# Hybrid decoder step on one core: dense split in place, merged gathers, earlier pick matrix, reordered end

## The reference

```python
# layer 0: RG-LRU mixer, memory attention, dense SwiGLU; layer 1: gated DeltaNet, memory attention, experts
for i in range(DEPTH):
    mix = rglru(x) if i % 2 == 0 else gated_delta(x)
    x = layer_norm(ALPHA * x + mix)
    x = layer_norm(ALPHA * x + mem_attention(x))
    ff = swiglu(x) if i % 2 == 0 else moe_ffn(x)
    x = layer_norm(ALPHA * x + ff)

def moe_ffn(x):                      # top 2 of 8 experts, softmax over the two logits
    gate = sum(one_hot(top_i) * softmax(top_v))
    return sum(gate[:, e] * swiglu_e(x) for e in range(8))
```

## Time and profile before

| | us |
|---|---|
| timed runs, median of 3 (lowest to highest) | 2506.08 (2505.19 to 2506.25) |
| the profiled execution | 2509.16 |
| its span, first to last instruction | 2507.3 |

### The profile page before, as it was taken

How to read it: one execution, slowest core, us unless ns; L and a number is a source line. 1 busy time by engine, 2 the same in 40 slices (tenths; PEclk the granted TensorE clock), 3 DMA queues, 4 the chain that set the end, 5 groups by cost and what they waited for, 6 DMA issues and landing times.

```text
span 2507.3 us, 43919 instructions
## 1 busy us (share of the span) xinstructions
PE 2291.6 (91%) x17238; PEld 2165.0 (86%) x17238; DVE 1134.6 (45%) x1739; ACT 720.5 (29%) x1218; POOL 1063.6 (42%) x1483
## 2 busy tenths in 40 slices
PE   8998889899999998999999778888799999999993
PEld 8988867899999996888888667867699999999993
DVE  3684412411011147777777644412557777410004
ACT  2352321311001114333333311321355666411103
POOL 4657434588888875433333105534221232100001
PEclk9999899899999998999999988999699999999996
DMA  7214442222222222211121102541176777778884
GB/s 296 100 60 162 154 165 85 93 84 84 89 88 84 89 90 69 69 55 62 62 63 63 45 27 88 194 165 68 52 256 208 260 249 264 238 247 280 285 285 161
DMA packets 98515, 347.22 MB, mean 138 GB/s; under 512 B 13488, under 2 KB 18864, under 8 KB 93472
## 3 DMA queue, kind: packets, MB, share of 16 engines
q1 hardware_dynamic: 73136, 279.08, 31.9%
q10 hardware_dynamic: 19472, 45.28, 5.2%
q0 software_dynamic: 5728, 20.38, 2.2%
HBM read 318.25 MB, written 26.47 MB: 137 GB/s over the span
## 4 chain that ended last, share of the span: by engine, by line
PE 64%; issue 15%; DVE 9%; POOL 6%; ACT 3%; DMA 3%; ACTq 0%; DVEq 0%; POOLq 0%; SPq 0%
PE ps L625 26%; PE ps L1262 8%; PE ps L1235 6%; PE ps L865 4%; PE ps L1264 4%; POOL wl L531 3%; PE ps L1252 3%; POOL wh L527 2%; DMA raw<-weights 2%; PE ps L726 1%; DVE x L1953 1%; PE ps L1076 1%; PE ps L1072 1%; PE ps L1055 1%; PE ps L730 1%
## 5 line engine op out<-in xcount | busy, mean ns | idle before, releaser
L527 POOL TENSOR_TENSOR wh<-raw,tab 128x256 fp32r<-128x256 f32 x672 | 438.8, 684 | 807.4 <-PE ps L625 543.5
L531 POOL TENSOR_TENSOR wl<-raw,wh 128x256 fp32r<-128x256 f32 x672 | 522.1, 808 | 0.0
L625 PE MATMUL ps<-xh,wh 128*128 128x272 f32 x2048 | 306.5, 300 | 47.1 <-POOL wl L531 15.5
L625 PEld LDWEIGHTS ps<-xh,wh 128*128 128x128 f32 x2048 | 276.8, 195 | 61.9 <-issue 24.5
L625 PE MATMUL ps<-xh,wl 128*128 128x272 f32 x2048 | 298.7, 296 | 0.0
L625 PE MATMUL ps<-xl,wh 128*128 128x272 f32 x2048 | 281.0, 289 | 0.0
L625 PEld LDWEIGHTS ps<-xh,wl 128*128 128x128 f32 x2048 | 277.1, 195 | 1.8 <-issue 0.5
L625 PEld LDWEIGHTS ps<-xl,wh 128*128 128x128 f32 x2048 | 266.2, 189 | 0.0
L1262 PE MATMUL ps<-moe_x,moe_wh 128*128 128x416 f32 (+3 forms) x768 | 214.5, 356 | 4.8 <-DVE moe_wl L2458 3.5
L2458 DVE TENSOR_TENSOR moe_wl<-raw,moe_wh 128x1024 fp32r<-128x1024 f32 x144 | 178.1, 1237 | 52.1 <-ACT moe_wh L1832 49.1
L1264 PE MATMUL ps<-moe_x,moe_wl 128*128 128x208 f32 (+3 forms) x768 | 188.9, 246 | 0.0
(11 more groups left out here) (407 smaller groups left out, 3901.4 us busy)
## 6 DMA issues: line engine op xcount, KB each, us to landing
raw<-weights SPq DMA_DIRECT2D x488, 512.0 KB, 4.2
moe_h<-cache SPq DMA_DIRECT2D x6, 2048.0 KB, 8.6
moe_h<-cache ACTq DMA_DIRECT2D x4, 2048.0 KB, 14.9
work<-cache SPq DMA_DIRECT2D x4, 2048.0 KB, 8.0
moe_h<-rows_x POOLq DMA_DIRECT2D x12, 512.0 KB, 8.1
rows_x<-lnsq ACTq DMA_DIRECT2D x9, 512.0 KB, 11.1
work<-scratch ACTq DMA_DIRECT2D x16, 272.0 KB, 4.2
work<-cache ACTq DMA_DIRECT2D x2, 2048.0 KB, 10.4
```

The lines of the kernel that those rows point to most:

```text
L527: nc.gpsimd.tensor_tensor(flat(h1[:, k0:k1]), flat(r1[:, k0:k1]), one_col, MUL).then_inc(pool_hi, 1)
L531: low = nc.gpsimd.tensor_tensor(flat(l1[:, k0:k1]), flat(r1[:, k0:k1]), flat(h1[:, k0:k1]).bitcast(F), SUB)
L625: last = mm(ps[:, 2 * i + h, 0:HT], w[:, par_, k, :], a[:, k, h * HT:(h + 1) * HT], start=(n == 0 and k == 0), stop=(n == 2 and k == KT - 1))
```

## The change

The change has four parts.

Split in place: `wl` now lies on `raw`, so the low part overwrites the tile that it was made from, and `wh` has four tiles. Every load waits for `w_used` of four tiles back. In the query, output, feed-forward and delta-net-output groups (`ahead=True`) `split` waits for the load alone; elsewhere it stays two tiles behind PE. The down loop of the feed-forward is written out twice, since its slot index now depends on the turn.

```diff
-RAW, SPLIT, PIECES = 4, 2, 4
+RAW, PIECES, PACE = 4, 4, 2
...
-        wh = sb("wh", [P, SPLIT, KT, P], R)
-        wl = sb("wl", [P, SPLIT, KT, P], R)
+        wl = nc.alloc_sbuf_tensor_at("wl", [P, RAW, KT, P], R, offset=nc.sbuf_base - 4 * RAW * KT * P)
+        wh = sb("wh", [P, RAW, KT, P], R)
...
-                    if offset is None:
-                        ge(sp, w_used, t * RAW + (j + 1 - RAW))
-                    else:
-                        ge(sp, w_split, t * RAW + (j + 1 - RAW - offset))
+                    ge(sp, w_used, t * RAW + (j + 1 - RAW))
...
                     pool.wait_ge(w_in[j], t * 16 + 16)
-
-                    ge(pool, w_used, t * RAW + (j + 1 - SPLIT - (first if j < SPLIT else 0)))
-                    h1, l1, r1 = wh[:, j % SPLIT], wl[:, j % SPLIT], raw[:, j]
+                    if not ahead:
+                        ge(pool, w_used, t * RAW + (j + 1 - PACE - (direct if j < PACE else 0)))
+                    h1, l1, r1 = wh[:, j], wl[:, j], raw[:, j]
...
-            turns(S_Q[0], 16, 4, 20)
-            turns(S_FFN, HALVES * 36, 4, 24)
-            turns(S_GDN, 4 * GH + 8, 4, 28)
-            turns(S_Q[1], S_MOE - S_Q[1], 4, 32)
+            turns(S_Q[0], 16, 4, 20, ahead=True)
+            turns(S_FFN, HALVES * 36, 4, 24, ahead=True)
+            turns(S_GDN, 4 * GH, 4, 28)
+            turns(S_GDN + 4 * GH, 8, 0, 28, ahead=True)
+            turns(S_Q[1], S_MOE - S_Q[1], 4, 32, ahead=True)
```

```diff
+                    if r == NE - 1:
+                        continue
                     pool.wait_ge(m_ye, KT * (r + 1))
                     pool.dma_start(rows_y[b:b + P, :], M_y[:, 0, :]).then_inc(m_out, 16)
...
-                pool.wait_ge(m_out, OUT_BY[NE - 1])
+                pool.wait_ge(m_x, NE - 1)
+                pool.wait_ge(m_out, OUT_BY[NE - 2])
...
-                            out=Y_in[tt][m][0:n, :], out_offset=None, in_=rows_y,
-                            in_offset=bass.IndirectOffsetOnAxis(ap=R_slot[0:n, m, tt:tt + 1], axis=0)).then_inc(c_in_y[tt], 16)
+                            out=Y_in[tt][m][0:n, :], out_offset=None, in_=rows_y[0:BASE[NE - 1], :],
+                            in_offset=bass.IndirectOffsetOnAxis(ap=Z_slot[0:n, m, tt:tt + 1], axis=0)).then_inc(c_in_y[tt], 16)
...
+            def last_products(tt):
+
+                n = P if tt < NC else NS
+                for hf in range(2):
+                    if tt >= 2:
+                        pe.wait_ge(c_stat, tt - 1)
+                    last = mm(ps[0:n, 4 + 2 * (tt % 2) + hf, :], Z_turned[:, tt * P:tt * P + n], M_y[:, 0, 512 * hf:512 * hf + 512],
+                              start=True, stop=True)
+                last.then_inc(r_pe, 1)
...
+                    if r == NE - 1 and f == 4:
+                        dve.wait_ge(r_pe, SHARED_T + 1)
+                        s(V.tensor_copy(Z_turned[:, 0:TP], ps[:, 6, :]))
+                        s(V.tensor_copy(Z_turned[:, TP:T], ps[:, 7, 0:NS]), r_dve, SHARED + 2)
+                    if r == NE - 1 and f >= FT - NT:
+                        combine(f - (FT - NT))
```

```diff
-                    if tt:
-                        columns(tt - 1)
+                    if tt >= 2:
+                        columns(tt - 2)
+                columns(NT - 2)
                 columns(NT - 1)
...
-                    for m in range(2):
-                        s(V.scalar_tensor_tensor(z, Y_in[tt][m][0:n, :], R_w[0:n, tt, 1 - m:2 - m], z, MUL, ADD))
+                    dve.wait_ge(r_pe, SHARED_T + tt + 2)
+                    z = T_x[0:n, tt, :].rearrange("p (a b) -> p a b", b=512)
+                    s(V.tensor_tensor(z, z, ps[0:n, 4 + 2 * (tt % 2):6 + 2 * (tt % 2), :], ADD))
```

More of the change, by code:

```diff
@@ L42 @@
 ZEROS = -(-ROWS // P)
+SHARED, SHARED_T = 11, 6
 PICKED, GATHERED = 6, 2
@@ L869, in one @@
                     pe.sem_inc(passed, 1)
[L870 to L875 removed]
+                    down(0)
+                    down(1)
                 repeat(pe, n, one)
@@ L1869, in columns @@
                 n = P if tt < NC else NS
-                for hf in range(2):
+                for hf in range(2 if tt < 2 else 1):
                     act.wait_ge(c_tr, 2 * tt + hf + 1)
```

152 lines of the change are left out of this document (100 added, 52 removed).

## The result

The changed kernel takes 2488.5 us in the median (2487.3 to 2493.4) beside 2505.6 us for the kernel before (2504.3 to 2506.3). The ratio is 0.9936 with a 95% interval of 0.9919 to 0.9953: 16 us are won, between 12 and 20. Forecast were 36 us and 2470.2, with a range of 2456 to 2485; the time lies above the range. The sign is right, the size is half.

The account below looks back on a forecast made before the run. TensorE (PE) was taken as busy nearly throughout, so only waits and lower-clock time could be won. Terms 27.6 + 4.5 - 0.5 - 9.2 - 1.0 + 14.5 = 35.9 us, from 2506.08 to 2470.2, range 2456 to 2485.

Parts of the forecast that it names:

- The openings, 6.2 + 6.4 + 10.0 + 3.3: Us won by splitting ahead at openings of first query projection, feed-forward, delta net's output and second query projection, in turn.
- What is late next: Loads now wait for PE's use; behind an opening 0 to 3.5 us lost, 1.7 taken in delta net's output, nothing elsewhere.
- GpSimd is quicker than PE wherever it may run on: From a dense feed-forward stretch: GpSimd splits a tile in 5.33 us, PE takes 6.02 us for it.
- The output projections, 3.2: Attention output projections in both layers: eight tiles in 48.2 us in place of 49.85, 1.6 won each.
- Low parts beside GpSimd, 1.5: VectorE's eight low parts per opening slow down beside running GpSimd; 0.5 us lost in each of three openings.
- The rival with a whole GpSimd operation per low part: Port costs more: each opening low part loses about 0.7 in place of 0.29 us; 2484 us, chance 0.07.
- Pick matrix, 4.5: Picks made before VectorE's branch let PE start earlier and spare its clock; 4.5 us won, bounds 2.7 to 8.4.
- The share matrices: VectorE's some 26 small operations behind the branch; 0 to 3 us may stick out, 0.5 taken as loss.
- Gathers, 9.2 + 1.0: Last expert: 4.46 MB of gathered rows delay weights by 9.2 us, and PE's five transposes cost 1.0.
- a halving of the rate, 7.3: Last expert: queues served packet by packet give gathers and weights half of 393 GB/s each, costing PE 7.3 us.
- The end, 14.5: After the last row copy: PE multiplies shares at once, fewer VectorE additions; 14.5 us won, bounds 10 to 16.
- that running ahead doesn't show: Rival: PE's third tile in the opening waits for something else, splitting ahead gives only 5; 2493 us, chance 0.06.
- The slower rival: In-place subtraction costs GpSimd more and it sets the pace of 112 tiles; 2750 us if doubled, chance 0.04.

Follow-up runs that it names:

- e10: Changed kernel with all tiles of the running-ahead matrices split ahead and GpSimd stopping before each attention output projection; 2479.6 us, 0.9881 of the kernel before.
- e12: Changed kernel with all tiles split ahead, GpSimd's stop, delta-net output's third and fourth tiles split after head 6, gathers spread; 2472.5 us, 0.9848 of the kernel before.
- e4_paced: Changed kernel with the gathers spread over the last expert and VectorE's additions moved to match; 2486.3 us, 0.9912 of the kernel before.
- e6: Changed kernel with all tiles split ahead and VectorE's 128x256 copy written as a maximum of its source with itself; 2494.1 us, 0.9963 of the kernel before.
- e8: Changed kernel with all tiles split ahead, copy as maximum, delta-net output's third and fourth tiles split after head 6, gathers spread; 2482.1 us, 0.9908 of before.

## Why the prediction was half right

1. **The openings, 6.2 + 6.4 + 10.0 + 3.3: right, in one place with luck.** Measured 6.9, 6.1, 8.8 and 2.0. "What is late next" was the right question: the load behind an opening is late, but in the first query projection (1.15) and not in the output of the delta net, where the 1.7 for it was taken. There the step "GpSimd is quicker than PE wherever it may run on" failed: beside VectorE's work a tile's split takes 6.59 and not 5.33, the five tiles take 32.69 as before, and the 2.5 counted for them didn't come. That 10.0 was near is partly luck: a gain of 2.5 and a loss of 1.7 were counted, and neither came.
2. **The output projections, 3.2: wrong, by a misread diff.** The step "GpSimd no longer waits for PE" was carried from the first `split` of a group to its loop, which doesn't get `ahead`. `e10` shows that the price was about right (1.5 and 1.6; in `e12` 1.8 and 1.6), for an edit that wasn't made.
3. **The early split of the delta net's output costs 3.2 to 6.6 us in head 5: left out.** The prediction took the 115 us in which GpSimd sat idle as free room. It asked what GpSimd's work does to VectorE in the openings and not where else the split would now run: through a chain in which PE waits for VectorE. 3.2 us are VectorE's longer operations, the rest PE's clock, which fell in six of the seven traces. Seven traces against seven show the loss.
4. **The start-up, 1.7 to 5.2 us: left out.** The part on loads ("nothing elsewhere") looked at steady running and openings. The in-place split changes when every load starts, from the first matrix on, and it was not followed past ScalarE's queue. Why the issuing there takes longer is not shown.
5. **Low parts beside GpSimd, 1.5: about right.** The eight of an opening take 8.72 us, 1.09 each in place of 0.73, and PE's three openings in the first trace are 0.6 shorter, 0.3 longer and 0.9 longer, together some 0.7 longer. The rival with a whole GpSimd operation per low part is out.
6. **Pick matrix, 4.5: right** within its bounds, measured 6.0: 3.6 by the earlier start, 2.5 by the clock. The share matrices show no cost (0.5 taken).
7. **Gathers, 9.2 + 1.0: right** in the mean (10.6), 13.1 in the first trace; of this the transposes are some 0.1 and not 1.0. The price per MB from an earlier expert's start carried over; a halving of the rate, 7.3, would have been too little.
8. **The end, 14.5: right**, 14.2.

The fall in the first pair of traces is 15.5 us: 6.6 for head 5, 4.9 for the output projections, 1.7 for the start-up, 2.9 for the last expert, 2.5 less in the output of the delta net and the second query projection, 1.6 in the two experts ahead of the last, against 3.3 more in the stretch of the pick matrix and the experts up to the fifth, and 1.4 more in all the rest. The range failed because nearly all of it went one way: points 2 and 3 alone make 11.5 us, and neither was among the rivals. Two rivals come equally near in time, 4.5 us off: that the port costs more (2484) and that running ahead doesn't show (2493). Neither is what happened: in the openings the port cost less than was taken, and running ahead shows in all four. The port's is the nearer in kind, since VectorE beside GpSimd's split is what costs head 5. The slower rival is out: GpSimd's low part in place takes 0.70 a piece beside an idle VectorE (2.81 for four). Of the signs of being wrong that the prediction named, two came: a load late behind an opening, and the last expert 13.1 us longer in the first trace (9.4 to 11.5 in the six others with the burst).

## What to carry to other kernels

When an engine is allowed to run ahead, look up in the trace what the other engines do at the place where its work will now fall; its idle time there is free only if nothing there slows down beside it. Read a helper's every call for the new argument before pricing what it does. Here a burst of transfers under a weight stream cost about what its bytes cost in the nearest such place of the trace, and spreading it gave back only part, 2.7 of 10.6 us.

## What was not expected of the hardware

- A VectorE copy of 128x256 elements takes 0.29 us with GpSimd idle, 0.66 beside a split that began after a pause, and 10.1 to 10.8 beside a row of splits without a pause, until 0.15 us after the row's end. A two-input maximum of the same shape took 10.0 to 10.4 (`e6`, `e8`). But VectorE's low parts of 128x544, eight in a row, take 1.09 each in the openings beside such a row, and one alone in the feed-forward took 14.4 to 14.6. So the shape alone doesn't decide; what decides whether an operation gets a turn, the runs don't tell. The Trainium skill, SBUF — State Buffer, section "Who interferes with whom", says of a VectorE operation that takes both port pairs, of which GpSimd shares one: "Whoever issues first gets the shared pair for the whole instruction; the other fully blocks (not throttle)." The copy's 0.29 against 0.66 agrees with that, though no run shows which ports this copy takes; that an operation is passed over by sixteen instructions in a row goes beyond it.
- Where PE works in short pieces (heads 5 to 7), the granted clock can differ between executions of the same code. Two traces of one program agree (heads 6 and 7: 108.5 and 108.5 us before, 108.7 and 109.4 after), but `e4_paced`, with the changed kernel's code there, ran head 5 at 1.00 and not 0.94, 3.4 us faster, and heads 6 and 7 in 106.4 us. Over all fourteen traces heads 6 and 7 take 106.3 to 114.2 us, the longest with 30 us near 0.50. So a single trace can be some us off there.
